# A fourth weight block in each quarter of the first stage, and a quarter of a modulation vector moved from VectorE to TensorE

## The reference

```python
mod = silu(c) @ mod_w + mod_b                 # (1, 6*2048): six vectors
sh_m, sc_m, gt_m, sh_f, sc_f, gt_f = split(mod, 6)
h = rms_norm(x, g0) * (1 + sc_m) + sh_m
q, k, v = split(h @ w_qkv)                    # 2048 -> 2048 + 512 + 512
y = window_attention(rope(q), rope(k), v, sinks) @ w_o
x = x + gt_m * rms_norm(y, g1)
h = rms_norm(x, g2) * (1 + sc_f) + sh_f
x = x + gt_f * rms_norm((silu(gate(h)) * up(h)) @ w_out, g3)   # hidden 5632
```

## Time and profile before

| | us |
|---|---|
| median of 3 runs | 1133.84 |
| lowest and highest | 1131.18, 1135.58 |
| the profiled execution's own time | 1133.45 |
| its span, first to last instruction | 1131.7 |
| mean granted clock of TensorE, share of full | 0.980 |
| PE busy in the span | 1068.3 |
| DVE, ACT busy | 687.1, 485.6 |

### The profile page before, as it was taken

One profiled execution on the slowest core, in us unless ns is written; L12 is line 12 of the kernel. 1 busy time (PEld: TensorE's weight loads), 2 busy tenths in 40 slices (PEclk: granted clock), 3 DMA queues, 4 the chain that ended last, 5 costly groups with the idle time before them and its releaser, 6 DMA issues.

```text
span 1131.7 us, 13640 instructions
## 1 busy us (share of the span) xinstructions
PE 1068.3 (94%) x4968; PEld 847.3 (75%) x4968; DVE 687.1 (61%) x870; ACT 485.6 (43%) x619; POOL 29.3 (3%) x39
## 2 busy tenths in 40 slices
PE   5788899899998799999999999999999999999996
PEld 2555766577786688888888888888888888888885
DVE  2686776878887836676675444445443545544456
ACT  4322456546763653333333433333334444334443
POOL 0000000000010100000000000000001000000000
PEclk9899999999998899999999999999999999999999
DMA  9999999988896426787785555555555455555542
GB/s 364 416 417 417 418 371 384 409 348 290 317 359 259 149 97 258 278 312 279 261 315 208 186 186 201 189 186 199 185 186 186 153 201 202 187 185 190 199 167 74
DMA packets 50599, 288.23 MB, mean 255 GB/s; under 512 B 6401, under 2 KB 6401, under 8 KB 23937
## 3 DMA queue, kind: packets, MB, share of 16 engines
q1 hardware_dynamic: 47090, 268.47, 63.4%
q0 software_dynamic: 2304, 16.78, 3.7%
q10 hardware_dynamic: 1168, 2.49, 0.6%
HBM read 285.36 MB, written 2.10 MB: 254 GB/s over the span
## 4 chain that ended last, share of the span: by engine, by line
PE 78%; DVE 9%; DMA 7%; ACT 3%; issue 3%; SPq 0%; POOL 0%; DVEq 0%; ACTq 0%; POOLq 0%
PE ps L1290 24%; PE ps L1292 24%; PE ps L1291 24%; DMA mraw<-in_mod_w 4%; DMA graw<-in_mod_h 3%; PE ps L1313 3%; DVE mraw L746 3%; DVE wlo L735 2%; ACT whi L396 2%; PE ps L1347 1%; PE ps L1447 1%; PE ps L1323 1%; PE ps L1336 0%; DVE wlo_in L735 0%; DVE guT L1155 0%
## 5 line engine op out<-in xcount | busy, mean ns | idle before, releaser
L735 DVE TENSOR_TENSOR wlo<-raw,whi 128x1024 fp32r<-128x1024 f32 x336 | 396.4, 1221 | 311.8 <-ACT whi L396 311.6
L1290 PE MATMUL ps<-whi,hThi 128*128 128x512 f32 x1232 | 489.5, 397 | 22.5 <-DVE wlo L735 18.5
L396 ACT ACTIVATE whi<-raw 128x2048 fp32r<-128x2048 f32 x168 | 321.5, 1915 | 396.5 <-PE ps L1292 381.5
L1291 PE MATMUL ps<-wlo,hThi 128*128 128x512 f32 x1232 | 483.9, 393 | 0.0
L1292 PE MATMUL ps<-whi,hTlo 128*128 128x512 f32 x1232 | 483.4, 392 | 0.0
L1290 PEld LDWEIGHTS ps<-whi,hThi 128*128 128x128 f32 x1232 | 233.8, 190 | 88.6 <-issue 36.1
L1292 PEld LDWEIGHTS ps<-whi,hTlo 128*128 128x128 f32 x1232 | 233.9, 190 | 49.7
L1291 PEld LDWEIGHTS ps<-wlo,hThi 128*128 128x128 f32 x1232 | 234.2, 190 | 47.5
L746 DVE CUSTOM_DVE_ANT_0 mraw<-mraw,cb,mbias 128x1024 f32<-128x1024 f32 x64 | 82.5, 1304 | 49.9 <-DMA mraw<-in_mod_w 49.9
L746 DVE CUSTOM_DVE_ANT_0 mraw<-mraw,cb,modT 128x1024 f32<-128x1024 f32 x64 | 81.4, 1282 | 21.8 <-DMA mraw<-in_mod_w 21.8
L1290 PE MATMUL ps<-whi,oThi 128*128 128x512 f32 x112 | 46.7, 417 | 6.6 <-DVE wlo L735 6.6
(11 more groups left out here) (151 smaller groups left out, 530.3 us busy)
## 6 DMA issues: line engine op xcount, KB each, us to landing
raw<-in_w_in SPq DMA_DIRECT2D x88, 1024.0 KB, 4.8
mraw<-in_mod_w SPq DMA_DIRECT2D x128, 512.0 KB, 8.0
raw<-in_w_out SPq DMA_DIRECT2D x44, 1024.0 KB, 4.8
raw<-in_w_qkv SPq DMA_DIRECT2D x24, 1024.0 KB, 11.8
graw<-in_mod_h SPq DMA_DIRECT2D x16, 1024.0 KB, 14.3
graw<-in_mod_h POOLq DMA_DIRECT2D x16, 1024.0 KB, 8.9
raw<-in_w_o SPq DMA_DIRECT2D x16, 1024.0 KB, 7.0
x<-in_x ACTq DMA_DIRECT2D x2, 1024.0 KB, 8.9
```

The source lines that it names most:

```text
L396: A(split_of(q, s)[0], raw[:, s], ACT.Copy).then_inc(hi_done, 1)
L735: V.tensor_tensor(low[:, k], raw[:, s, k], high[:, k].bitcast(F32), ALU.subtract).then_inc(done, 1)
L1290: mm(dst, hi, high[:, n], start=start, stop=False)
L1291: mm(dst, hi, low[:, n], start=False, stop=False)
```

## The change

- Each quarter takes a fourth block: slot 3 of quarter c is query group 1. Its bank of PSUM is shared with `sums`, so its result is taken out by ACT in each quarter (`q1_part`, into `q1a`, `q1b`, `q1c`) and added up by DVE (two additions over 128x1024 and `q1_total`). The blocks are numbered anew: 0 to 15 in the quarters (k, q0, v, q1), 16 to 23 two further query groups, 24 to 39 as before.
- In the quarters `hi` of a quarter's first block now stands ahead of `hThi` on ACT, and the first half of `lo` ahead of `h_lo` on DVE.
- The first quarter of sh_f goes by PE: a ninth group, `gate_sums(32)` to `gate_sums(35)`, `columns(8)`, `gate_mod(4)`; 8 mods less, 88 in place of 96 ahead of the feed-forward.
- The orders of SP, ACT, DVE and PE from the quarters to block 36 are written anew. Mods 32 to 50 stand ahead of `lo_of(27)`, 51 to 83 between `lo_of(27)` and `lo_of(36)`, 84 to 87 behind it. Before, these were 32 to 70, 71 to 92, 93 to 95.

```diff
@@ PE, quarters
             for c in range(4):
                 pe.wait_ge(h_ready, c + 1)
-                for e in range(3):
-                    g = 3 * c + e
...
+                project(c, c, hThi, hTlo, 0, half_done, slot=0)
+                if c < 3:
+                    sums(c + 1, (0,))
+                project(c, c, hThi, hTlo, 2, half_done, slot=1)
+                if c < 3:
+                    sums(c + 1, (1,))
+                    project(c, c, hThi, hTlo, 4, half_done, slot=2, halves=(0,))
+                    sums(c + 1, (2,))
+                    last_q(c, 0)
+                    sums(c + 1, (3,))
+                    project(c, c, hThi, hTlo, 4, half_done, slot=2, halves=(1,))
+                    columns(c + 1)
+                    last_q(c, 1)
@@ PE, behind them
+            project(3, 3, hThi, hTlo, 4, half_done, slot=2, halves=(0,))
+            k_turn()
+            project(3, 3, hThi, hTlo, 4, half_done, slot=2, halves=(1,))
+            last_q(3, 0)
+            q_turn(0)
+            last_q(3, 1)
+            scores(0)
+            q_block(16, (0,))
+            gate_sums(16)
+            q_block(16, (1,))
...
+            gate_sums(29)
+            o_block(24, (0,))
             gate_sums(30)
+            o_block(24, (1,))
             gate_sums(31)
             o_block(25, (0,))
+            gate_sums(32)
+            columns(7)
+            gate_sums(33)
             p_turn(2)
+            gate_sums(34)
             o_block(25, (1,))
+            gate_sums(35)
             q_turn(3)
             outputs(2)
+            columns(8)
             o_block(26, (0,))
@@ ACT, quarters
             sums_out(0)
+            hi(0, 0)
             for c in range(4):
                 act.wait_ge(hf_done, c + 1)
                 A(hThi[:, 4 * c:4 * c + 4], nT[:, 4 * c:4 * c + 4], ACT.Copy).then_inc(hhi_done, 1)
...
+                hi(c, 1)
+                if c < 3:
+                    hi(c, 2)
+                    hi(c, 3)
+                    q1_part(c, 0)
+                    sums_out(c + 1)
+                    hi(c + 1, 0)
+                    q1_part(c, 1)
@@ DVE, quarters
                 modulate(c)
+                lo(c, 0, (0,))
                 h_lo(c)
-                lo_of(3 * c)
+                lo(c, 0, (1,))
@@ DVE, output stage
             lo_of(34)
-            mods(88, 3)
+            mods(77, 4)
             lo_of(35)
-            mods(91, 2)
+            mods(81, 3)
             lo_of(36)
-            mods(93, 2)
+            mods(84, 3)
@@ SP, output stage
             load_block(37)
-            load_mods(89, 3)
+            load_mods(78, 3)
             sp.wait_ge(oT_ready, 8)
             for b in range(HB):
                 sp.dma_start(x1[:, b], x[b * P:(b + 1) * P, :]).then_inc(x1_in, 16)
             load_block(38)
-            load_mods(92, 3)
+            load_mods(81, 4)
             load_block(39)
-            load_mods(95, 1)
+            load_mods(85, 3)
```

More of the change, by code:

```diff
@@ new lines, in _ @@
+            hi_of(18)
+            normalise(0, 0)
+            normalise(0, 1)
+            sums_out(4)
+            hi_of(19)
+            pT_out(0)
+            qT_out(1)
+            oT_out(0)
+            evac_q(2, 0)
+            hi_of(20)
+            probs(1, 0)
+            evac_q(2, 1)
+            hi_of(21)
+            probs(1, 1)
+            hi_of(22)
+            normalise(1, 0)
+            normalise(1, 1)
+            sums_out(5)
+            hi_of(23)
+            pT_out(1)
+            qT_out(2)
@@ L911, in _ @@
+            next(keys)
             lo_of(14)
-            mods(36, 1)
+            next(keys)
+            first_q = rope_parts(1, half_evac, 4, qs0, qr[:])
+            next(first_q)
             lo_of(15)
-            mods(37, 1)
+            next(first_q)
+            mods(33, 1)
+            q1_total(0)
+            lo_of(16)
+            q1_total(1)
             max_and_sinks(0, 0)
             max_and_sinks(0, 1)
-            mods(38, 1)
-            denominator(0, 0)
-            lo_of(16)
@@ L920, in _ @@
-            mods(39, 1)
-            rope_q(1)
-            lo_of(17)
-            denominator(0, 1)
-            gate_mod(0)
-            mods(40, 3)
-            lo_of(18)
-            mods(43, 3)
+            lo_of(17)
+            mods(34, 1)
+            denominator(0, 0)
+            mods(35, 1)
+            rope_q(1)
+            denominator(0, 1)
+            lo_of(18)
+            mods(36, 2)
+            lo_of(19)
+            gate_mod(0)
+            mods(38, 1)
             oT_lo(0)
-            lo_of(19)
@@ L947, in _ @@
+            lo_of(23)
+            gate_mod(1)
             oT_lo(1)
-            lo_of(23)
-            mods(58, 3)
+            mods(43, 1)
+            lo_of(24)
             max_and_sinks(2, 0)
             max_and_sinks(2, 1)
-            mods(61, 3)
+            mods(44, 2)
             denominator(2, 0)
-            lo_of(24)
-            mods(64, 2)
+            mods(46, 1)
+            denominator(2, 1)
+            lo_of(25)
             rope_q(3)
-            lo_of(25)
-            denominator(2, 1)
+            mods(47, 2)
@@ L960, in _ @@
+            gate_mod(2)
+            lo_of(26)
+            mods(49, 2)
+            oT_lo(2)
             gate_mod(3)
-            mods(66, 3)
-            lo_of(26)
-            mods(69, 2)
-            oT_lo(2)
+            gate_mod(4)
             lo_of(27)
-            mods(71, 2)
             max_and_sinks(3, 0)
             max_and_sinks(3, 1)
+            mods(51, 3)
+            denominator(3, 0)
             lo_of(28)
-            mods(73, 3)
-            denominator(3, 0)
+            mods(54, 3)
@@ L1057, in _ @@
             lo_of(37)
-            mods(95, 1)
-            dve.wait_ge(half_evac, 16)
+            mods(87, 1)
+            dve.wait_ge(half_evac, 14)
             dve.wait_ge(ysq, 4)
@@ L1514, in _ @@
+            q_block(22, (1,))
+            scores(2)
+            gate_sums(27)
+            q_block(23, (0,))
+            gate_sums(28)
+            q_block(23, (1,))
+            columns(6)
+            gate_sums(29)
+            o_block(24, (0,))
             gate_sums(30)
-            q_block(22, (0,))
-            scores(2)
-            q_block(22, (1,))
+            o_block(24, (1,))
             gate_sums(31)
-            q_block(23)
-            o_block(24)
-            columns(7, 0)
             o_block(25, (0,))
+            gate_sums(32)
```

421 lines of the change are left out of this document (204 added, 217 removed).

## The result

The changed kernel is slower: 1153.93 us (median of 4 runs, 1153.21 to 1155.51) against 1133.92 for the kernel before on the same chip (4 runs, 1131.18 to 1135.58). The ratio is 1.0189, 95% interval 1.0163 to 1.0215. The forecast was 1132.7, range 1122 to 1143. The profiled execution took 1155.51 us, the highest of the four; its span is 1153.6, 21.9 more than before.

A forecast was written before the change was run, and what follows sets the result against it. It took PE's work plus its holes to set the front, DMA engines close behind, and PE alone from 405 us. Terms -5.0 + 4.9 - 4.4 + 2.5 + 1.2 = -0.8 gave 1132.7 us, range 1122 to 1143.

The forecast's parts named there:

- Step 1: Quarters up to quarter 3's start: 17.2 us of added PE work costs 12.3 us through shorter gaps; -5.0 us.
- Step 2: The ninth group on PE: four `gate_sums` and one `columns`, where nothing hides them; +4.9 us.
- stage B: The window from quarter 3 to block 26, 151.9 us in the kernel before; not the rival B.
- Step 3: PE's waits from quarter 3 to block 26: 6.6 us against 11; -4.4 us (-9 to +8).
- Rival C: Quarter 3 to block 26: gate loads land as before, 8.9 us, in closer spacing; sum +11.5, 1145 us; chance 0.09.
- Step 4: Block 26 to 36: 33 mods fill DVE and DMA engines, taken as 73 us; +2.5 us (-3.9 to +9).
- Rival B: Output stage becomes DVE's and the loads', at `lo_of(31)` to `lo_of(36)`; sum +6.5, 1140 us; chance 0.18.
- Step 5: Behind block 36: four mods among `lo` 36 to 39 in place of three; +1.2 us (0 to +3).
- C stayed: Here C is the window from block 26 to block 36, 70.4 us in the kernel before; not the rival C.

The follow-up runs named there:

- e7: e1 with the split of each quarter's first block put back behind `hThi` (ACT) and `h_lo` (DVE); 1145.96 us.
- e10: The kernel before with only the reordered split of each quarter's first block and the sine tables' arithmetic moved forward; 1131.66 us.
- e2: The changed kernel without the ninth group, that quarter of the shift left zero; 1140.26 us.
- e8: e1 with four of the seven mods ahead of `oT_lo(2)` moved behind `lo_of(27)` to `lo_of(30)`; 1134.60 us.
- e3: The changed kernel with mods 51 to 83 loading 16 of 128 rows, their arithmetic unchanged; 1142.36 us.
- e4: The changed kernel with mods 51 to 83 multiplying 64 of 1024 columns, their loads unchanged; 1145.12 us.
- e1: The changed kernel with 14 of the 33 mods moved ahead of `oT_lo(0)`, `oT_lo(1)` and `oT_lo(2)`, SP's order following; 1132.57 us.
- e6: e1 with gate loads 18 to 35 bringing 16 of 128 rows, so gate and shift are incomplete; 1120.06 us.
- e9: The changed kernel without the ninth group (96 mods), mods spread as in e1 but four moved from ahead of `oT_lo(2)` to behind `lo_of(27)` to `lo_of(30)`; 1135.14 us.

## Why the prediction was wrong

**Step 1 held in its mechanism.** Gaps of 2.89 us against 3.0, quarter 3 at 137.58 against 135.8. The difference from the forecast is within what this stage does by itself: eleven runs of the same code put the start at 133.0 to 138.0. I gave the gain to the shorter chain; e7 and e10 show that it takes chain and fourth block together.

**Step 2 was costed rightly as work and too cheaply as a part.** Four sums and `columns` are 4.9 us, but without them e2's stage B is 15.8 us shorter. Its four loads stand where the spacing was closest already.

**Step 3 failed in two terms, the landing and the clock.** Its forecast was 4.6 us of gate waits, from a landing of 6.7 us, which I took from the stage's mean DMA load (80%). The share did fall, to 0.82, and the landing stayed at 8.6. The mean hides where the slack lies. The engines have it up to 170, around 200 and from 272 on, and are full where the closest sums stand:

```profile
150.00:160.00 10.00, 10.00 (x54) 8.44 (x53) 8.65 (x10) 6.27 (x8) 0.00 (x0) 1.00 0.66 239
190.00:200.00 10.00, 10.00 (x80) 6.78 (x79) 3.40 (x5) 4.68 (x6) 0.54 (x1) 1.00 0.72 272
250.00:260.00 10.00, 7.95 (x34) 5.13 (x36) 6.93 (x10) 3.06 (x5) 0.57 (x2) 0.83 1.02 425
260.00:272.00 12.00, 6.98 (x49) 3.41 (x42) 2.55 (x5) 2.06 (x4) 1.07 (x2) 0.87 1.01 405
```

That a load lands by what is queued at its moment is the likely reading and not shown: in e8, with 2 MiB moved away, the median is 8.6 again. The waits were 11.3, the longest at sums 34 (3.0) and not at 33 (2.0). By the prediction's own spacings, 3.8 us for sums 34 against 4.8 for 33, a landing of 4.4 or 5 us would have held 34 by 0.9 to 1.0 us too, which it left out for both. Work at 1.2 GHz came behind the last ones, as these two rows of PE in after show (sums 34, whose eight matmuls took 1.07 at 2.4 GHz, and the first matmul of a half, 0.50 there):

```profile
269.79 1.93 PE L1395 MATMUL ps<-graw,ccz 128*32 128x512 f32 x8 [3.03 <-DMA graw<-in_mod_h]
271.65 0.80 PE L1338 MATMUL ps<-whi,oThi 128*128 128x512 f32 x1
```

The mean clock of B is 0.96, at most 5.8 us of 144.7, where I had kept none. Rival C had the landing right; it took +8 for step 3, and +5.1 came, with 11.3 us of gate waits where it had 17.

**Step 4 failed most, by 11.8 us.** The step put 70.5 us of DVE beside 70.5 us of loads and took 73 for both. The sizes were near: DVE was busy for 67.9 us, and the stage moved 328 GB/s x 84.8 us = 27.8 MB, 66.7 us at 417 GB/s, where the step had 29.4 MB. The overlap failed: DVE waited 14.9 us for loads on top of its work. With four slots of `mraw` a late load is idle time of DVE and a late mod is idle time of the DMA engines, so the two add in part (e3 75.5 and e4 80.5 alone, 84.8 together). The step also let the loads run at 417 GB/s from the start; in the first 10 us of the stage they ran at 116. That is harmless by itself, since e1 begins with 116 GB/s too and takes 66.0 with 19 mods; what it costs with 33 mods was not measured alone. And the lead that 25 us less of DVE work in B should have given could not be used, since `oT_lo(2)` stood ahead of the mods. That DVE would be idle there was to be read in the diff: 19 mods stand ahead of `lo_of(27)` where there were 39, two of them between `lo_of(26)` and `oT_lo(2)`, and nothing behind these can start before PE's `outputs(2)`. Rival B named the place, `wlo` of block 31, and that is where PE's 7.3 us are; its price (+9) left out the start, and its chance (0.18) assumed that slack ahead of the stage helps. The upper end of my range for step 4, +9, was "DVE's waits stay as they are on top of its work"; they went from 7.8 to 14.9.

**Step 5 held:** +0.8 against +1.2; and the loops from the first `norm_turn` on kept their 757 us.

**B and C came together.** The prediction gave them as alternatives and set its range by one at a time. B adds 7.3 us to the forecast's sum of -0.8 and C adds 12.3; both together are +18.8, or 1152.3 us, against +21.9 in the profiles and a median of 1153.93. That this comes near is partly luck, as B's +9 for step 4 stood for +14.3 and C's +8 for step 3 for +5.1. The two have separate causes: with 5.1 us less of gate waits C stayed at 85.8 (e2), and with 11.3 less it stayed at 66.0 (e6 against e1).

**Could it have been faster?** Not in any arrangement of the whole work that was tried. e1, e8, e9 and e10 are all within 0.25% of before, with block 36 at 343 to 350. Up to there the bytes are the same in all of them: in before 405 x 123.55, 373 x 151.9 and 335 x 70.4 make 130 MB, in e1 406 x 135.77, 365 x 148.0 and 318 x 66.0 make 130 too (windows from 0 on); at 417 GB/s they are 312 us. So at most the remaining 34 us can be won by order, and PE's own work and first loads take an unknown part of them. e6, with gate loads of an eighth, is the one kernel clearly below before (0.9891), so part of what is left may lie there (or in its fewer bytes); whether a third slot for them would give it was not tried.

## What to carry to other kernels

Before moving work from one stage to the next on an engine with a fixed order, find the first instruction in that order that waits for another engine, and count what stands ahead of it: work behind it gives no lead, and loads that wait for its slots stop as well. What cost here was the crowd behind that instruction, and not the idle time in front of it. If arithmetic and loads would each fill a stage and few slots lie between them, put a price on their waiting for each other: here 84.8 us came where either alone gave 75.5 and 80.5. The landing time of a load is to be read where the load will be issued; a measured one is safer than one scaled by a mean share.

## What was not expected of the hardware

**The length of a gap alone does not decide the clock behind it.** Quarter 1 begins behind the same wait of 2.89 us in after and in e8, whose code up to there is the same. In after the granted clock fell and the first matmul took 0.79 us, in e8 it stayed at 2.4 GHz and took 0.50. The window of that quarter in e8, against the second one of after at the top (33.55 us at 0.91):

```profile
71.78:102.59 30.81, 27.92 (x136) 19.18 (x137) 21.95 (x34) 10.28 (x9) 0.00 (x0) 1.00 1.02 417
```

That is 2.7 us for one quarter, and with three quarters the spread of 5 us in quarter 3's start; the times of one kernel spread as far (e1 1128.92 to 1137.12 over 10 runs). A term of under 3 us in this stage can't be read from one profile.

**Landings did not follow size across the queues.** From 137 to 282 us in after, mods of 0.5 MiB landed after 9.4 us in the median, blocks of 1 MiB from the same queue after 7.6 and gate loads of 1 MiB from POOL's after 8.6. Mods stand behind blocks and other mods in SP's order, which may be why. In the same place of the same queue size does count: e6's gate loads of 16 rows landed after 4.5 us in the median (2.9 to 7.5), where e1's full ones took 8.8.
